# In-projection by token half in two banks, and the dilated heads' scores in groups of four, in a two-layer hybrid attention kernel

## What is computed

```python
def hybrid_layer(x, attn_norm, w_in, moba_out_norm, dil_out_norm, w_out, mlp_norm, w_up, w_down, cos, sin):
    proj = rms_norm(x, attn_norm) @ w_in
    qa, ka, va, qd, kd, vd = jnp.split(proj, [...], axis=-1)
    qa, ka, qd, kd = apply_rope(...)
    out_a = rms_norm(merge_heads(moba_attention(qa, ka, va)), moba_out_norm)
    out_d = rms_norm(merge_heads(dilated_attention(qd, kd, vd)), dil_out_norm)
    x = x + jnp.concatenate([out_a, out_d], axis=-1) @ w_out
    h = rms_norm(x, mlp_norm)
    return x + jnp.square(jax.nn.relu(h @ w_up)) @ w_down
```

## Time and profile before

| | |
|---|---|
| median of 3 runs | 599.85 us (599.79 to 599.92) |
| the profiled execution | 599.85 us; span of its instructions 598.1 us |
| TensorE busy | 589.3 us (99% of the span) |
| TensorE weight loads | 485.0 us (beside the matmuls) |
| VectorE busy | 393.9 us (66%) |
| ScalarE busy | 316.8 us (53%) |
| GpSimd busy | 46.5 us (8%) |
| DMA | 104.00 MB, mean 174 GB/s |

### The profile page before, as it was taken

One profiled execution on the slowest core, in us unless ns is written; L12 is line 12 of the kernel. 1 busy time (PEld: TensorE's weight loads), 2 busy tenths in 40 slices (PEclk: granted clock), 3 DMA queues, 4 the chain that ended last, 5 costly groups with the idle time before them and its releaser, 6 DMA issues.

```text
span 598.1 us, 8728 instructions
## 1 busy us (share of the span) xinstructions
PE 589.3 (99%) x3066; PEld 485.0 (81%) x3066; DVE 393.9 (66%) x655; ACT 316.8 (53%) x536; POOL 46.5 (8%) x51
## 2 busy tenths in 40 slices
PE   8999999999999999999999999999999999999995
PEld 5877777788888888888888777878888888888884
DVE  5866958687755755656388478677875755755634
ACT  5747749475535435344284567674654435435322
POOL 0220230110000000000004013001100000000001
PEclk9999999999999999999999999999999999999999
DMA  8954344248665464564266434431877465465301
GB/s 303 354 212 142 141 141 142 71 140 276 220 222 196 151 236 174 169 250 143 71 209 212 141 140 142 133 112 45 269 249 249 141 219 201 149 224 188 105 0 70
DMA packets 58842, 104.00 MB, mean 174 GB/s; under 512 B 1808, under 2 KB 35264, under 8 KB 58816
## 3 DMA queue, kind: packets, MB, share of 16 engines
q1 hardware_dynamic: 58320, 102.87, 50.7%
q10 hardware_dynamic: 496, 0.81, 0.4%
HBM read 102.62 MB, written 1.05 MB: 173 GB/s over the span
## 4 chain that ended last, share of the span: by engine, by line
PE 98%; DVE 1%; issue 0%; POOLq 0%; POOL 0%; ACT 0%; DVEq 0%; ACTq 0%
PE psum L1051 20%; PE psum L892 20%; PE psum L894 19%; PE psum L893 19%; PE psum L1054 10%; PE psum L1008 2%; PE psum L1024 1%; PE psum L899 1%; PE psum L999 1%; PE psum L985 1%; PE psum L983 1%; PE psum L882 1%; PE psum L1027 1%; PE psum L914 1%; PE psum L920 0%; PE psum L923 0%
## 5 line engine op out<-in xcount | busy, mean ns | idle before, releaser
L611 DVE TENSOR_TENSOR w_lo<-raw,w_hi 128x1024 fp32r<-128x1024 f32 x188 | 229.4, 1256 | 51.4 <-ACT w_hi L447 51.4
L447 ACT CAST w_hi<-raw 128x1024 fp32r<-128x1024 f32 x188 | 187.0, 1049 | 3.0 <-DMA raw<-in_w_in 3.0
L1051 PE MATMUL psum<-xt,w_hi 128*128 128x512 f32 x512 | 160.8, 395 | 0.0
L892 PE MATMUL psum<-w_hi,ot_hi 128*128 128x512 f32 x320 | 127.5, 398 | 0.0
L894 PE MATMUL psum<-w_hi,ot_lo 128*128 128x512 f32 x320 | 125.0, 391 | 0.0
L893 PE MATMUL psum<-w_lo,ot_hi 128*128 128x512 f32 x320 | 124.9, 390 | 0.0
L1054 PEld LDWEIGHTS psum<-xt,w_lo 128*128 128x128 f32 x512 | 96.2, 188 | 22.3
L1054 PE MATMUL psum<-xt,w_lo 128*128 128x256 f32 x512 | 100.8, 278 | 0.0
L1051 PEld LDWEIGHTS psum<-xt,w_hi 128*128 128x128 f32 x512 | 80.3, 189 | 2.3
L558 ACT COPY up_cross<-psum 128x512 f32<-128x512 f32 x32 | 18.8, 588 | 118.8 <-PE psum L1054 118.8
L892 PE MATMUL psum<-w_hi,xt 128*128 128x512 f32 x180 | 74.3, 413 | 0.0
(11 more groups left out here) (85 smaller groups left out, 445.5 us busy)
## 6 DMA issues: line engine op xcount, KB each, us to landing
raw<-in_w_up SPq DMA_DIRECT2D x32, 1024.0 KB, 5.5
raw<-in_w_down SPq DMA_DIRECT2D x32, 1024.0 KB, 6.7
raw<-in_w_in SPq DMA_DIRECT2D x21, 1024.0 KB, 5.5
raw<-in_w_out SPq DMA_DIRECT2D x8, 1024.0 KB, 4.9
raw<-in_w_in SPq DMA_DIRECT2D x3, 512.0 KB, 7.8
raw<-in_w_in SPq DMA_DIRECT2D x4, 256.0 KB, 4.6
out<-x SPq DMA_DIRECT2D x3, 256.0 KB, 2.4
raw<-in_w_in ACTq DMA_DIRECT2D x2, 256.0 KB, 5.1
```

Source lines behind the costliest of these rows:

```text
L447: act.copy(w_hi[:, slot, part], raw[:, slot, part]).then_inc(hi_done, 1)
L611: dve.tensor_tensor(w_lo[:, slot, part], raw[:, slot, part], w_hi[:, slot, part].bitcast(F32), ALU.subtract).then_inc(split_done, 1)
L892: pe.matmul(out, s_hi, m_hi, start=first, stop=False)
L1051: pe.matmul(up_banks[b][:, f, :], w_hi[:, slot, cols[f]], xt[:, k, :, :].rearrange("p a b -> p (a b)"), start=k == 0, stop=False)
```

## The change

It does three things.

*Projection by token half.* In groups 1 to 5, a step no longer takes one feature slice for both token halves. Steps 0 to 3 of a group do all eight slices of the first half (two slices a step), steps 4 to 7 those of the second. A step is still six matmuls. Each half has one bank, 2 or 3, used by all of the groups 1 to 5 in turn (`group_bank`); group 0 stays as it was, in banks 0 and 1. A half's products with the position tables, or its copy to v, are assigned to the step at which that half is full (`ROPE_AT`, `V_AT`), with a semaphore `half_done` for the first half. A group's units are all read twice, so they are released on the last four steps (`HI_AT` follows).

*Scores in groups of four.* Banks 0 and 1 are free after group 0, and serve as score banks for heads 2, 3, 6 and 7 (and 8, 9 as before). So heads 0 to 3 are scored together on step 22 (before: 23 and 27) and heads 4 to 7 on step 32 (before: 31 and 35), right behind the products of head pairs 0 and 1, which before stood on 31 and 35.

*Steps shifted.* The masks and what follows them are a step earlier for heads 0 to 3 and a step later for heads 4 to 7. Key tiles 2 and 3 are turned on steps 19 and 20. The products of pairs 2 and 3 are on 42 instead of 41.

```diff
-QK_AT = {23 + 2 * h if h < 8 else 38 + h: h for h in range(N_HEADS)}
+QK_AT = {22 + 2 * h if h < 4 else 24 + 2 * h if h < 8 else 38 + h: h for h in range(N_HEADS)}
 NORM_AT = {s + 1: h for s, h in QK_AT.items()}
 PT_AT = {s + 3: h for s, h in QK_AT.items()}
-PV_AT = {31: (0,), 35: (1,), 41: (2, 3), 53: (4, 5), 57: (6, 7)}
-QK_PAIRS_AT = {23: (0,), 27: (2,), 31: (4,), 35: (6,), 46: (8, 10), 50: (12, 14)}
+PV_AT = {32: (0, 1), 42: (2, 3), 53: (4, 5), 57: (6, 7)}
+QK_PAIRS_AT = {22: (0, 2), 32: (4, 6), 46: (8, 10), 50: (12, 14)}
...
-QKT_AT = {14: 0, 15: 1, 20: 2, 21: 3, 39: 4, 41: 5, 44: 6, 47: 7}
-ROPE_AT = {8 * g + 8: g for g in ROPE_GROUPS}
-V_AT = {8 * g + 8: g for g in V_GROUPS}
+QKT_AT = {14: 0, 15: 1, 19: 2, 20: 3, 39: 4, 41: 5, 44: 6, 47: 7}
+ROPE_AT = {8: ((0, 0), (0, 1))} | {8 * g + 4 * t + 4: ((g, t),) for g in ROPE_GROUPS if g > 0 for t in range(TOK)}
+V_AT = {8 * g + 4 * t + 4: (g, t) for g in V_GROUPS for t in range(TOK)}
...
-V_AT_LAST = max(V_AT)
-HI_AT = {s + int(s == V_AT_LAST): s // 2 + HI_AHEAD for s in range(0, 2 * ATT_UNITS, 2)}
+HI_AT = {s + int(s % 8 == 4 or s in V_AT): s // 2 + HI_AHEAD for s in range(0, 2 * ATT_UNITS, 2)}
...
-        early_banks = {8: banks[0], 9: banks[1], 12: banks[2], 13: banks[3]}
+        more_banks = {h: banks[h % 2] for h in (2, 3, 6, 7, 8, 9)} | {12: banks[2], 13: banks[3]}
...
+        def group_bank(g, t):
+
+            return banks[2 * int(g > 0) + t]
...
             def project_in(l, s):
...
+                t, j = s % 8 // 4, s % 4
+                u = 4 * g + j
+                if t == 0:
+                    unit_ready(l, u // 2, u % 2)
...
+                if j == 0 and g - 1 in V_GROUPS:
+
+                    pe.wait_ge(v_done, l * 4 + t + 1)
+                elif j == 0 and g > 1:
+                    pe.wait_ge(rope_terms, l * 8 + 2 * ROPE_GROUPS[g - 1] + t + 1)
+                tok = slice(t * P, (t + 1) * P)
+                for k in (2 * j, 2 * j + 1):
+                    cols = slice((k % 4) * BANK, (k % 4 + 1) * BANK)
+                    last = three(group_bank(g, t)[:, :], xt[:, k, 0, tok], xt[:, k, 1, tok],
+                                 w_hi[:, u // 2 % RING, cols], w_lo[:, u // 2 % RING, cols], k == 0, k == KT - 1)
+                if t == 1:
+                    last.then_inc(weights_used, 1)
+                elif j == 3:
+                    last.then_inc(half_done, 1)
...
             def score_pair(l, h):
...
-                if h == SET_HEADS:
-                    pe.wait_ge(rope_terms, l * 8 + 8)
+                if h == 2:
+                    pe.wait_ge(rope_terms, l * 8 + 2)
...
-                elif h >= 2:
-                    pe.wait_ge(masked, l * N_HEADS + h)
+                elif h == SET_HEADS:
+                    pe.wait_ge(masked, l * N_HEADS + SET_HEADS)
+                elif h >= 4:
+                    pe.wait_ge(masked, l * N_HEADS + h - 2)
```

More of the change, by code:

```diff
@@ L507, in _ @@
                     if s in V_AT:
-                        g = V_AT[s]
-                        act.wait_ge(weights_used, used(l, 4 * g + 3))
+                        g, t = V_AT[s]
+                        if t == 0:
+                            act.wait_ge(half_done, half_group(l, g))
+                        else:
+                            act.wait_ge(weights_used, used(l, 4 * g + 3))
                         act.wait_ge(rstd_done, l * STATS + ST_X + 1)
[L511 to L514, removed]
+                        act.activation(v[:, V_GROUPS[g], t, :], group_bank(g, t)[:, :], ACT.Copy,
+                                       scale=rstd[:, ST_X, t:t + 1]).then_inc(v_done, 1)
                     if s in QKT_AT:
@@ L663, in rope_products @@
                     dve.wait_ge(rope_done, l * 8 + 2 * (j - 1) + t + 1)
-                bank = banks[2 * (g % 2) + t]
+                bank = group_bank(g, t)
                 cos, sin, neg = (rope_r[:, t, n * HALF:(n + 1) * HALF] for n in range(3))
@@ L732, in _ @@
                                  (exp_done, l * N_HEADS + h + 1))
-                        bank = early_banks.get(h, s_banks[h % 2])
+                        bank = more_banks.get(h, s_banks[h % 2])
                         dve.tensor_tensor_reduce(out=scores[:, h % 2, 0:P], in0=bank[:, 0:P], in1=m[:, P:2 * P],
@@ L742, in _ @@
                     if s in ROPE_AT:
[L743 removed]
+                        if s == min(ROPE_AT):
                             scale_rope(l)
[L745 to L746 removed]
+                        for g, t in ROPE_AT[s]:
+                            rope_products(l, g, t)
                     if s % 2 == 1 and u < 2 * FIRST_UP + 1:
@@ L940, in project_in @@
-                if g == 0:
-                    pe.wait_ge(turned_lo, l * TRS + TR_X + k + 1)
-                if k == 0 and g in (2, 3, 5):
-                    pe.wait_ge(rope_terms, l * 8 + 2 * ROPE_GROUPS[g - 2] + 2)
-                if k == 0 and g == 1 and l == 0:
-                    pe.wait_ge(gains_kept, 1)
-                if k == 0 and g == 4:
-                    pe.wait_ge(v_done, l * 2 + 1)
+                elif k % 2 == 0:
+                    unit_ready(l, u // 2, u % 2)
+                pe.wait_ge(turned_lo, l * TRS + TR_X + k + 1)
@@ L949, in project_in @@
                 for t in range(TOK):
                     tok = slice(t * P, (t + 1) * P)
-                    last = three(banks[2 * (g % 2) + t][:, :], xt[:, k, 0, tok], xt[:, k, 1, tok],
-                                 w_hi[:, c % RING, cols], w_lo[:, c % RING, cols], k == 0, k == KT - 1)
-                    if t == TOK - 1 and s % 2 == 1:
-                        last.then_inc(weights_used, 1)
+                    last = three(group_bank(0, t)[:, :], xt[:, k, 0, tok], xt[:, k, 1, tok],
+                                 w_hi[:, u // 2 % RING, cols], w_lo[:, u // 2 % RING, cols], k == 0, k == KT - 1)
@@ L956, in project_out @@
+                if k % 2 == 1:
+                    last.then_inc(weights_used, 1)
             def project_out(l, acc, k, u, t, n, first, last):
```

33 lines of the change are left out of this document (21 added, 12 removed).

## The result

The changed kernel takes 616.08 us (615.71 to 616.83, 5 runs); the kernel before, on the same chip, 599.92 us (599.79 to 600.14, 5 runs). The ratio is 1.0271, 95% interval 1.0257 to 1.0285: slower by 16.2 us, where +8.85 was forecast. The sign was right, and the time lies 3.6 us above the upper end of the range.

The account below looks back on a forecast made before the run. TensorE, busy 589.3 of 598.1 us, was taken as the bound. A layer summed to -1.02 + 4.45 + 1.0 = +4.43 us, two to +8.85, giving 599.85 + 8.85 = 608.7 us, range 603.5 to 612.5.

Parts of the forecast that it names:

- Merged bursts: Attention stage, scores and products on steps 22 and 32: merging the dilated heads' bursts gains 0.925 us a layer.
- an exit: Around steps 38 to 42, three bursts in place of four save one burst exit, 0.1 us a layer.
- Projection by token half: Projection matmuls, groups 1 to 5: as many, same shape and reads, so the new order costs 0.
- The guess at weights and banks: Projection halves: weights ready with 0.9 us of cover, banks back in time, cost 0; rival of lateness 0.05, 610.7 us.
- I see no stall there: Emptying of the projection banks by rope products or the copy of v: no wait of TensorE, 0.
- The collision: Steps 39 and 41: query tile and probabilities share `t_bank`, so TensorE waits for ScalarE's copy, at least 1.0 us each.
- The standstill on step 39: Step 39: TensorE waits 4.45 us a layer for ScalarE's copy, queued behind head 7's exponentials and a cast.
- the list between them holds as much now as then: VectorE, from head 4's mask to head 7's: the same work as before, which took 11.39 us.
- T + 14.0: Step 39: when the probabilities could follow the query tile, T being the last projection matmul of step 32.
- The clock: Behind step 39's standstill: a clock fall would cost 1.78 us each time, 3.55 in all, 612.2 us; rival, chance 0.14.
- The argument against it from the earlier trace: Granted clock 1.00 in every stretch read, also the first 2 us with 1.70 us without a matmul: no fall shown.
- the fall on one layer only: Variant of the clock rival: the clock falls behind step 39's standstill in one layer only, 610.4 us.

Follow-up runs that it names:

- experiment 1: Changed kernel's projection by token half alone, with score, product and transpose tables of the kernel before and the step 52 cast not moved: 602.03 us, ratio 1.0033.
- (2): Projection by token half alone, as above, with the position products of group 4's first half moved from step 36 to 38: 600.18 us, ratio 1.0001.
- experiment 5: Changed kernel, two runs: step 38's weight cast moved to step 39, 614.54 us; or position products of group 4's first half moved to step 38, 612.95 us.
- experiment 3: Kernel before with query tile 4 turned on step 40 instead of 39, where head 7's probabilities are turned: 601.72 us, ratio 1.0031.
- experiment 4: Changed kernel with 18 matmuls that nothing reads, between the two groups of transposes on step 39: 612.97 us, ratio 1.0219.
- last run of experiment 5: Changed kernel with the position products of group 4's first half on step 38 instead of 36: 612.95 us, ratio 1.0212.
- experiment 7: Step 52's weight cast moved back from step 53: in the changed kernel 617.14 us; in that kernel with 18 filling matmuls on step 39, 611.57 us.
- experiment 6: Changed kernel with query tiles 4 and 5 turned elsewhere: on steps 40 and 43, 611.39 us; on steps 36 and 38, 604.32 us.

## Why the prediction was right or wrong

*Merged bursts, -0.925 a layer and an exit of 0.1: right.* The burst of step 32 takes 62.97 - 59.34 - 0.455 = 3.175 us, against 3.19.

*Projection by token half, 0: wrong.* The guess at weights and banks held; none of the waits named there came. What failed is "I see no stall there": I asked when banks and weights are wanted, and not what else stands in VectorE's list where half of the position products went. Alone it costs 2.1 us (experiment 1) and nothing with the products two steps later (2). In the changed kernel it is no term of its own; it is 1.17 us of the standstill (5), with GpSimd's addition that came along, and the 0.23 us of step 31.

*The collision, 1.0 us: right* in both kernels that show it alone, 1.01 on step 41 and 1.8 for two in experiment 3.

*The standstill on step 39, 4.45 us: right in its mechanism, 4.83 in size.* The chain ran as counted to within 0.01 us at head 4's mask and was 0.99 us late at head 7's. The step that failed here is "the list between them holds as much now as then": the operations are the same, but not what runs beside them. GpSimd's additions met two scalings and held VectorE for 1.84 us, where the old row held 1.03 on two weight splits. On the other side TensorE was itself 0.57 us later than counted (73.91 against T + 14.0), mostly by the wait on step 37. By luck the two partly cancelled, and 0.38 us was left.

*The clock: wrong, and the largest single step.* "So it is a rival and not in the sum", the step that put the clock's cost at nothing, failed: behind the standstill the granted clock was 0.55, and the matmuls 0.43 us apart, on both layers. It cost 3.1 us by experiment 4, where the rival had 3.55 from the first matmuls of the program. I gave it 0.14 because no row showed a standstill of that length inside the stream; that absence said nothing either way, and the first matmuls did run 0.43 us apart. The Trainium skill (TensorE: Matmul & The Clock Gate, "The HAM clock gate") has idleness put the clock back; the traces here agree for each standstill of 3.41 to 4.6 us, and show no fall after one of 1.72 us. The argument against it from the earlier trace rows was weak: that window shows 1.00 while the matmuls right behind it were slow, and so does a window over those matmuls (1.70 to 5.30 us), so it could not speak for the clock. The size of 1.78 us for each time was no more than a fair guess: the standstills measured here cost 1.6 us (both layers of the changed kernel) to 2.7 (second layer of the last run of experiment 5). With the fall on one layer only, its own terms give 610.5 us, not 610.4.

*Not in the sum at all: the small waits,* 1.3 us a layer and 0.6 once, 3.2 us. The sum held them at nothing, without a look at those steps. Three of them (steps 31, 37, 55) stand before transposes of probabilities. On 37 and 55 it is one pattern: a copy out of `t_bank` behind exponentials or a cast that had moved next to it. On 31 it is VectorE's scaling, held beside a GpSimd addition, and on 19 an addition of GpSimd itself. I had followed ScalarE's list over steps 37 to 39 only, where the diff also shifted it on others.

The errors add up: 3.1 (clock) + 3.2 (small waits) + 0.8 (standstill) = 7.1 of the 7.4 us between 608.7 and 616.08. The range stopped at 612.5 because its cases were taken one at a time; the clock and the small waits came together. What is not settled is where the last 0.3 us lies, and why the stretch of slow matmuls is eight long in one place and eleven in another; no run tried these apart. The causes of the waits on steps 19, 31 and 37 are read from the timelines; only that of step 55 was tested by a run (experiment 7).

## What to carry to other kernels

When a step moves, follow the in-order list of every helper engine over all the steps that shift, not only where the bound engine waits: a 1 us item set ahead of a mask or a copy came back as 1 us of standstill, several times here. Where the bound engine is TensorE and a forecast holds a standstill of several microseconds in its stream, the slow matmuls behind it belong in the sum, and a run that fills the gap with idle work measures them; here they cost 1.6 to 2.7 us for each standstill of 3.4 to 4.6 us. And before giving an idea up, change where its collision falls: two entries of a table recovered 11.8 of 16.2 us, and another layout of the same merging ended below the kernel before.

## What was not expected of the hardware

- The clock fell behind each standstill of 3.41 to 4.6 us, in four kernels and both layers of each, and behind waits of 0.81 and 2.17 us with nine matmul starts between them (experiment 6). It did not fall behind 1.72 us, nor behind 0.77 or 0.86. The slow stretch held 8 to 11 distances, most of 0.43 us, and cost 1.6 to 2.7 us; in experiment 6 it held at least five.
- Run times spread where the clock fell: 612.84 to 616.04 in experiment 5, against 612.65 to 613.32 with the gap filled. What an edit elsewhere gives can be hidden by it, as in experiment 7.
- VectorE's scaling of probabilities (one operation of 128x128 and one of 128x256, from SBUF) took 1.60 us beside GpSimd's addition and 0.55 without it. The first of the two took 1.35 us of it (0.29 alone) and ended at 74.22, the addition at 74.13. The weight splits beside an addition end 1.08 to 1.09 us behind it in three traces (before, experiments 1 and 2), and one alone takes 1.21. So an estimate from these rows is that VectorE's operation hardly moves until GpSimd's has ended. Not every operation is held: position products, which read one input from PSUM, keep their 0.42 us beside an addition (63.96 and 64.29 in the trace before). The Trainium skill (GPSIMD Engine Reference, "1. Specifications") says that GpSimd shares its SBUF interfaces with VectorE, with contention for VectorE instructions in a 2-port perf mode or with two SBUF inputs. The traces agree for the split, which has two SBUF inputs (1.98 us beside the addition, 1.22 alone), and for the products, which have one. The scaling has one too; whether it runs in such a mode no run here shows.
